# Ending the products ahead of two norms token tile by token tile, in a fused transformer kernel on one core

## The reference

```python
# layer 0, for latent and context tokens (4 token tiles)
h = h + g1 * ((y_conv, y_attention) @ w_out)
h = h + g2 * swiglu(rms_norm(h, norm2_g) * (1 + sc2) + sh2)   # the norm "f"
# layer 1
a = rms_norm(h, norm1_g) * (1 + sc1) + sh1                    # the norm "o"
p = a @ w_in      # cq, dq for 2 token tiles; ck, cv, dk, dv for 4
swiglu(x) = (silu(x @ w1) * (x @ w3)) @ w2                    # hidden width 2816
```

## Time and profile before

| | |
|---|---|
| runs shown | 2064.36 us median of 3 (2060.88 to 2065.09) |
| the profiled execution | 2061.86 us, span 2060.0 us |
| mean granted clock of TensorE | 0.902 |
| busy, share of the span: PE, PEld, DVE, ACT, POOL | 87%, 72%, 60%, 40%, 6% |

### The profile page before, as it was taken

How to read it: one execution, slowest core, us unless ns; L and a number is a source line. 1 busy time by engine, 2 the same in 40 slices (tenths; PEclk the granted TensorE clock), 3 DMA queues, 4 the chain that set the end, 5 groups by cost and what they waited for, 6 DMA issues and landing times. The chain is left out here.

```text
span 2060.0 us, 21353 instructions
## 1 busy us (share of the span) xinstructions
PE 1789.2 (87%) x8622; PEld 1485.9 (72%) x8622; DVE 1246.3 (60%) x1716; ACT 823.7 (40%) x996; POOL 116.7 (6%) x116
## 2 busy tenths in 40 slices
PE   4988999699799995859767999999987899878997
PEld 2766777487678884749646888888867866668986
DVE  5455782377545535554636888888875555555643
ACT  5222231422113224222314777677744433525532
POOL 1310001000100011320010000000000000000000
PEclk8897988799999997975676999999998999998999
DMA  6322331255545432210033888888855521125552
GB/s 277 102 102 93 132 125 39 102 189 184 194 158 204 163 113 73 84 67 13 1 137 109 326 324 332 324 325 324 322 197 179 176 93 40 62 94 194 183 194 102
DMA packets 61146, 332.54 MB, mean 161 GB/s; under 512 B 16804, under 2 KB 17379, under 8 KB 27890
## 3 DMA queue, kind: packets, MB, share of 16 engines
q1 hardware_dynamic: 55792, 321.54, 42.8%
q10 hardware_dynamic: 4354, 6.32, 0.9%
q0 software_dynamic: 896, 3.26, 0.4%
HBM read 329.96 MB, written 1.13 MB: 161 GB/s over the span
## 5 line engine op out<-in xcount | busy, mean ns | idle before, releaser
L1840 DVE TENSOR_TENSOR wlo__69<-raw__68,whi__70 128x2048 fp32r<-128x2048 f32 (+3 forms) x64 | 136.1, 2127 | 93.4 <-ACT whi__70 L1339 93.4
L1840 DVE TENSOR_TENSOR wlo__65<-raw__64,whi__66 128x2048 fp32r<-128x2048 f32 (+4 forms) x55 | 123.4, 2244 | 76.3 <-ACT whi__66 L1339 76.3
L1840 DVE TENSOR_TENSOR wlo__61<-raw__60,whi__62 128x2048 fp32r<-128x2048 f32 (+4 forms) x56 | 108.6, 1939 | 86.2 <-ACT whi__62 L1339 86.2
L1339 ACT ACTIVATE whi__70<-raw__68 128x2048 fp32r<-128x2048 f32 (+3 forms) x64 | 114.1, 1783 | 115.1 <-DMA raw__68<-in_ffn_w 47.9
L1339 ACT ACTIVATE whi__66<-raw__64 128x2048 fp32r<-128x2048 f32 (+4 forms) x55 | 100.0, 1818 | 77.0 <-DMA raw__64<-in_ev_w_in 21.6
L1339 ACT ACTIVATE whi__62<-raw__60 128x2048 fp32r<-128x2048 f32 (+4 forms) x56 | 91.2, 1628 | 72.8 <-DMA raw__60<-in_ev_w_in 20.7
L2757 POOL TENSOR_TENSOR keep__58<-keep__58,keep__59 128x1 f32<-128x1 f32 (+3 forms) x48 | 45.4, 948 | 1199.3 <-DVE keep__58 L1912 1199.3
L1339 ACT ACTIVATE whi__141<-raw__139 128x2048 fp32r<-128x2048 f32 (+2 forms) x16 | 28.1, 1754 | 126.9 <-DMA raw__139<-in_ffn_w 126.9
L860 PE MATMUL ps<-ffn__120,wlo__140 128*128 128x512 f32 x176 | 70.3, 399 | 9.8 <-DVE wlo__140 L1840 7.0
L1840 DVE TENSOR_TENSOR wlo__140<-raw__139,whi__141 128x2048 fp32r<-128x2048 f32 (+2 forms) x16 | 33.5, 2092 | 72.5 <-ACT whi__141 L1339 72.4
L2095 DVE TENSOR_REDUCE keep__58<-ps 128x1 f32<-128x256 f32 (+1 forms) x104 | 56.6, 544 | 28.5 <-PE ps L862 21.7
(11 more groups left out here) (1069 smaller groups left out, 5376.7 us busy)
## 6 DMA issues: line engine op xcount, KB each, us to landing
raw__217<-in_moe_w SPq DMA_DIRECT2D x24, 1024.0 KB, 6.6
raw__221<-in_moe_w SPq DMA_DIRECT2D x24, 1024.0 KB, 6.7
raw__225<-in_moe_w SPq DMA_DIRECT2D x16, 1024.0 KB, 5.7
raw__68<-in_moe_w SPq DMA_DIRECT2D x16, 1024.0 KB, 6.3
raw__64<-in_moe_w SPq DMA_DIRECT2D x16, 1024.0 KB, 6.8
raw__60<-in_ada_w SPq DMA_DIRECT2D x15, 1024.0 KB, 5.8
raw__64<-in_ada_w SPq DMA_DIRECT2D x15, 1024.0 KB, 5.7
raw__68<-in_ffn_w SPq DMA_DIRECT2D x14, 1024.0 KB, 4.9
```

The lines of the kernel that those rows point to most:

```text
L1339: e.activation(t.hi(), t.raw(), ACT.Copy).then_inc(*did("hi", i))
L1840: e.tensor_tensor(t.lo(), t.raw(), t.hi().bitcast(F32), ALU.subtract).then_inc(*did("lo", i))
```

## The change

- The second halves of the output projection and of block 1's ff2 are made by `proj_by_token`: token by token, over all row blocks, with all weight tiles of the half held. The weight tiles become free at the last token.
- The norm's steps follow each token (`norm_by_token` on ACT, likewise in DVE's and POOL's order), with `ahead` at 1 until the first pass is over. Four buffers for scaled tokens instead of two.
- TensorE turns the first two tokens, begins the next stage with them, and turns the other two later: in the FFN the first pair of tiles is made in two halves of 256 tokens (`feat_halves`), in the odd mixer the second turning goes between cq and dq.
- Products wait for the pass by row block (`normed(N, p, k)`).
- The banks come from rings "x" (0 to 3) and "y" (4 to 7) there.
- The 11 small DMAs go to after the FFN's last ff3 product, the tables and the lambda to between the two halves of the last ff2, ACT's Exp in front of the second norm.
- `slot_f` is opened after the first pair of tiles. `in_use` tells the planner the oldest tile still held at an event.

```diff
-        "f": dict(after=("o", 0), free=[("prod", "o", 0, 1, 3), ("res", ("o", 0), 1, 3)],
-                  xs=XSf * 2, tm=TMf, out=AT4f, tiles=4, mod=[
+        "f": dict(after=("o", 0), free=[("prod", "o", 0, 1, 3)], xs_free=[("pv", "a0", 31)], xs=XSf, tm=TMf, out=AT4f, tiles=4, mod=[
...
         busy = max([i for i in range(max(n - 4, 0), n) if not TILES[i].sums], default=0)
+        busy = min([busy] + [in_use[event] for event in events if place[event] == n])
...
-    def normed(N, p):
-        return [(f, N, p, k0) for k0 in range(0, KT, 2) for f in ("nhi", "nlo")]
+    def normed(N, p, k):
+
+        return [(f, N, p, k - k % 2) for f in ("nhi", "nlo")]
...
+        def proj_by_token(key, x, nt, K, src, n, ready, ring):
+
+            kc, tiles = 2048 // n, []
+            for t in range(nt):
+                b = take(ring, *key, t)
+                for k in range(K):
+                    if t == 0 and k % kc == 0:
+                        tiles.append(use(src[k * 128:min(k + kc, K) * 128, :], min(kc, K - k), n))
...
+                    p = mm3(b[:, 0:n], x(k, t), sub((hi, lo), slice(None), k % kc), k == 0, k == K - 1)
+                    if t == nt - 1 and k % kc == kc - 1 and k < K - 1:
+                        p.then_inc(*done("part", *key, k - k % kc))
+                        consumed(tile, "part", *key, k - k % kc)
+                p.then_inc(*done("prod", *key, t))
+            consumed(tiles[-1][0], "prod", *key, nt - 1)
...
+        def feat_halves(parts, x, m, ready, ring, between):
...
+            for half in range(2):
+                o = slice(half * 256, half * 256 + 256)
+                if half:
+                    between()
+                for n, (key, src, f0) in enumerate(parts):
+                    if half == 0:
+                        held.append((*use(src[:, f0 * 128:(f0 + m) * 128], KT, m * 128),
+                                     [take(ring, *key, j) for j in range(m)]))
...
+                    if half:
+                        consumed(tile, "prod", *key, m - 1)
...
+        norm_turn("f", 0, "x")
...
+                feat_halves([(("ff1", 0, 0), W["ffn_w1"][0][:, bs], 0), (("ff3", 0, 0), W["ffn_w3"][0][:, bs], 0)], AT4f, 2,
+                            lambda half, k: normed("f", half, k), "7", lambda: norm_turn("f", 1, "y"))
...
+        norm_turn("o", 0, "x")
         for c0, w_, kind in ODD:
+            if kind == "dq":
+                norm_turn("o", 1, "y")
...
+        def norm_by_token(N, key):
+            at["ahead"] = 1
             for t in range(4):
-                feed(("prod", "o", 0, half, t))
...
+                feed(("prod", *key, 1, t))
+                if t < 3:
+                    norm_square(N, t)
+                if t == 1:
+                    norm_scale(N, 1)
+            norm_turned(N, 0)
+            at["ahead"] = 2
+            norm_square(N, 3)
+            norm_scale(N, 3)
+            norm_turned(N, 1)
...
         for s, n in due(("lam_s",)):
             e.wait_ge(s, n)
         e.activation(LM[:, 2:4], LM[:, 0:2], ACT.Exp).then_inc(*did("lam_e"))
+        norm_by_token("o", ("ff2", 1))
...
             for half in range(2):
+                if blk and half:
+                    for v in range(2):
+                        gain("n1b", sc1b, v, 6, 7)
+                    tables()
+                    at["ahead"] = 1
                 for t in range(4):
                     feed(("prod", "ff2", blk, half, t))
...
+                    if blk and half and t < 3:
+                        norm_scale("o", t)
         norm_turned("o", 0)
+        at["ahead"] = 2
         norm_scale("o", 3)
         norm_turned("o", 1)
```

More of the change, by code:

```diff
@@ L380, in _build @@
     A30 = A3.col
-    XSo, TMo = A3.some(2, 1024), A3.some(3, 512)
+    TMo = A3.some(3, 512)
+    assert A3.col <= slot_f_end
     A3.col = A30
@@ L534, in _build @@
         w["out_free"] = w["tm_free"] = w["free"]
-        w["xs_free"] = lambda t, N=N, w=w: w["free"] + ([("nt", N, 0, 6)] if t > 1 and w["tiles"] == 4 and N != "a" else [])
+        w.setdefault("xs_free", w["free"])
     def xn(N, t):
@@ L801, in done @@
             if book.counting:
-                place[name, *key] = state["tile"]
+                n = place[name, *key] = state["tile"]
+                in_use[name, *key] = next((i for i in range(max(n - 8, 0), n) if TILES[i].done is None), n)
             return did(name, *key)
@@ L896, in feat @@
                 for k in range(KT):
-                    for s, n in state["due"](*ready):
+                    for s, n in state["due"](*ready(k)):
                         e.wait_ge(s, n)
@@ L931, in gates @@
                         for k in range(k0, k0 + 4):
-                            for s, m_ in state["due"](*normed("s", 0)):
+                            for s, m_ in state["due"](*normed("s", 0, k)):
                                 e.wait_ge(s, m_)
@@ L1342, in norm_square @@
             w = NORM[N]
-            for s, n in due(*h_done(w["after"], t), *w["xs_free"](t)):
+            for s, n in due(*h_done(w["after"], t), *w["xs_free"]):
                 e.wait_ge(s, n)
@@ L1530, in scalar_program @@
                          *([("prod", "ff2", 0, 1, 3)] if blk else ()))
-            for half in range(2):
+            for half in range(1 if blk else 2):
                 for t in range(4):
                     feed(("prod", "ff2", blk, half, t))
-        over = [("prod", "ff2", 1, 1, 3)]
-        feed(*over)
-        for s, n in due(*over, ("res", ("ff2", 1), 1, 3), ("fhl", 1, 10)):
+        for s, n in due(("prod", "ff3", 1, 10, 0)):
             e.wait_ge(s, n)
@@ L2237, in vector_program @@
         for half in range(2):
+            if half:
+                for v in range(2):
+                    gain("n2a", sc2, v, 3, 4)
+                at["ahead"] = 1
             for t in range(4):
@@ L2244, in vector_program @@
                 empties(("o", 0, half, t), ("rt", ("o", 0), half, t))
-        for v in range(2):
-            gain("n2a", sc2, v, 3, 4)
-        norm_scale("f", 0)
-        norm_scale("f", 1)
+                if half and t < 3:
+                    norm_scale("f", t)
         norm_turned("f", 0)
-        norm_scale("f", 2)
+        at["ahead"] = 2
         norm_scale("f", 3)
@@ L2796, in gpsimd_program @@
                 residual(("o", 0), half, t, TMPa[(half * 4 + t) % 4])
-        for t in range(4):
-            norm_rsqrt("f", t)
+                if half:
+                    norm_rsqrt("f", t)
         for blk in range(2):
@@ L2804, in gpsimd_program @@
                     residual(("ff2", blk), half, t, TMPf[t])
-        for t in range(4):
-            norm_rsqrt("o", t)
+                    if blk and half:
+                        norm_rsqrt("o", t)
         TS5 = TS.rearrange("p (g i q h f) -> p g i q h f", g=4, i=2, q=2, h=2)
```

131 lines of the change are left out of this document (65 added, 66 removed).

## The result

| | before | changed |
|---|---|---|
| median of the runs on one chip | 2063.7 us (2060.88 to 2065.09, 4 runs) | 2033.5 us (2031.96 to 2038.01, 4 runs) |
| ratio of the times, 95% interval | | 0.986 [0.985, 0.988] |
| the profiled execution | 2061.86 us, span 2060.0 | 2032.86 us, span 2031.0 |
| mean granted clock of TensorE | 0.902 | 0.911 |

The change saves 30 us (29.0 in the spans of the two profiled executions). The predicted time was 2038.4 in a range of 2027 to 2050; it was built on the profiled execution (2061.9 less 23.5), so it compares with the 2032.86 of this table.

The account below looks back on a forecast made before the run. TensorE was taken to be held by chains of dependent steps at two norms, not a full engine. Gains of 13.8 and 15.5 less a 5.8 stall make 23.5 us: 2061.9 to 2038.4, range 2027 to 2050.

Parts of the forecast that it names:

- First head: From the last output product (time E) to the third FFN tile: 52.1 us before, 38.3 forecast, gain 13.8, bounds 10 to 18.
- token 3's square, root and scale come after it, 3.7 us: Ahead of the FFN: after the norm pass on two tokens (E+6.8), token 3 is scaled by E+10.5.
- Second head: From the last ff2 product (E') to dv's first: 60.7 us before, 45.2 forecast, gain 15.5, bounds 11 to 19.5.
- The third held tile: Last ff2 half: its conversion waits for tables and Exp; 3.5 us stall plus 2.3 cold start, cost 5.8, bounds 0 to 9.
- Row blocks "elsewhere 0, at most 1": At the other norms, the first product starts after its weight's low part, so waiting by row block gains 0, at most 1 us.
- The split "is nearly free": First FFN pair in halves: 192 products at 0.114, 21.9 us, against 96 at 0.227, 21.8.
- The sum: Whole kernel: gains 13.8 and 15.5 less cost 5.8 make 23.5 us, from 2061.9 to 2038.4.
- Cold starts: Rival, chance 0.12: three or four short gaps per head; three more cold starts at 2.3, 6.9 us, giving 2045.
- the rule that the prediction weighed: Waits between matmuls put TensorE at its low clock, so one long gap cut into several short ones can cost more.
- No stall at the third held tile: Rival, chance 0.14: if ACT converts that tile first, nothing waits in the last ff2 half; 2032.6.
- Tokens that fall behind on DVE: Rival, chance 0.07: conversions push two tokens past the end of the products, 2 x 4.9 us comes back; 2048.
- The slower case: Rival, chance 0.07: shared in-order DMA queue makes each of 21 later FFN pairs late by 1.5, 31.5 us lost; 2070.

Follow-up runs that it names:

- the run with both turnings together: Changed kernel with the second turning of the odd mixer's norm put back ahead of cq: 2033.3 us, dv 45.1 us after the last ff2 product.
- the two runs that undo it: Changed kernel with ACT's Exp put back behind the second norm: 2029.1 us; then DVE's tables also moved behind the third held tile's low part: 2027.2 us.
- the kernel with the first norm's part alone: Kernel before plus only the first norm's part; ff2, second norm, tables and small DMAs as before: 2039.3 us, ratio 0.989.
- the Exp late: Changed kernel with only ACT's Exp put back behind the second norm: 2029.1 us, ratio 0.984 to the kernel before.

## Why the prediction was right, and where it was off

**First head: 16.2 instead of 13.8.** The order of events was as told: tokens 0 to 2 hidden under the products, pass 1 to E+6.3 (told: 6.8), then token 3, then ff3's conversion, then the second half. The term that was mis-sized is "token 3's square, root and scale come after it, 3.7 us". It is 2.3: ACT is done with its part of the pass at 367.2 and squares token 3 while DVE still makes the last low part, so the scaling ends at E+8.6 instead of E+10.5, and ff3's low part at E+12.7 instead of E+14.7. These 2 us, 0.5 of them from the pass itself, run through to the end of the pair (E+36.1 against E+38.3, E now being 361.65; its first product on 256 columns was at E+3.5, told within 5). Two smaller things beside it: the last terms of the sum (29.1, 3.4 and 5.5) give E+38.0 and not 38.3, and the products of 256 columns come 0.120 us apart here, not 0.114 as in the earlier trace rows. The same in the second head: token 3 at E'+12.5, not 14.1, but there the fourth weight tile ends last and the early token gives nothing.

**Second head: 15.3 instead of 15.5.** First od tile's conversion at E'+0.2 (told 0.2), pass 1 to 10.3 (10.4), fourth tile landed at 20.6 (20.5), pass 2 to 30.1 (30.4), dv at 45.4 (45.2). The statement behind it, that the load of the fourth tile holds the second pass, is shown by the run with both turnings together, where the pass is moved out of its way and dv doesn't come earlier.

**The third held tile: 5.4 (5.9 by the products' starts) instead of 5.8.** The wait is 3.95 with 1.5 of low clock behind it; told were 3.5 and 2.3. So the sum is right because two terms miss in opposite ways. The wait is longer because the tables, told as 3.95 from before, took 5.04 in their new place beside POOL's addition; DVE came to them 0.4 earlier than told. And one thing wasn't in the prediction, though harmless: the tile lands not 4.2 us after its issue, as before, but 8.5, beside the 11 small DMAs. ACT would have been ready at 730.9 and waited for the Exp anyway. In the two runs that undo it this half is 3.4 and 5.9 us shorter.

**Row blocks "elsewhere 0, at most 1": right as far as a trace shows.** In the two heads they are worth 2.7 and 3.0 us, and the forecast had them in its terms for the passes. The median leaves 3.8 us more open, which the profiled execution doesn't have behind its second head.

**The split "is nearly free": nearly right.** Its 192 products, at 0.120 us, are 23.0 us against 21.8 for 96 whole ones, where the prediction had 21.9. It also brings nearly nothing in the first head as the change has it, 0.6 us, and nothing in the second (0.3 the other way). The prediction let a reader think that the half tiles hide the conversion; they do, but the work that is hidden would have fitted behind it.

**The sum: 29.0 instead of 23.5.** 2.4 of the 5.5 are the first head's, mostly token 3's term, 0.2 the two others together, and 2.9 lie where nothing was told: 0.7 before the first head, 0.2 in the FFN and 2.0 behind the second, of which one shorter wait is 1.1. That is within what unchanged code varies by from kernel to kernel, so this part is luck and not a term that the prediction lacked.

**The rivals.** Cold starts: the sum charged three low-clock stretches at 2.3 each, 6.9, and these three cost 5.4 (1.4 in the first head, 1.5 behind the stall, 2.5 at cq). A fourth, 2.3 at dv's first products, was there before too, with 2.5. Together 7.7 us, against 5.7 in the same places before; 1.5 of these 2 us are the stall's, which is a new wait, and only 0.5 come with the gaps cut in pieces. So the rule that the prediction weighed (the Trainium skill, "TensorE: Matmul & The Clock Gate", section "Loop structure matters more than you think") agrees with this trace in part: the low clock follows the waits of 2.42, 3.95 and 5.60 us, and none follows those of 1.62, 0.56 and 1.57 (in the kernel with the first norm's part alone it follows such a pair, 1.57 and 0.56). The 6.9 more of the cold rival are not there. No stall at the third held tile: ruled out by the wait itself, though the rival's time, 2032.6, is what the profiled execution took (2032.9); the time alone would have pointed to it. Tokens that fall behind on DVE: they were 3.8 us behind at token 0 (gate product at 349.16, its last product at 345.3) and had caught up at token 3 (362.05, 0.4 after E). The slower case, weight tiles late through the in-order queue: the FFN took 331.1 against 331.3. (The prediction counts 21 later pairs there; there are 11, of two tiles each, so 31.5 is the price of a delay for each tile.)

## What to carry to other kernels

When a chain of dependent steps stands between two dense stages, end the stage ahead of it piece by piece, and then ask of each engine's queue what stands in front of the step that ends last: here a 0.2 us Exp held a weight tile, a weight tile held token 3's half, and a chain held products that didn't need it. The reordering of the products won 30 us, and moving four such items of the queues won 16 more. An experiment that undoes one part must leave the assignment of buffers as it is; where the planner gave a tile to another slot, that alone cost 7 us. And single gains are best read from the stretch that was edited, as unchanged stretches move by 2 to 4 us between kernels and are counted in each gain.

## What the runs showed of the hardware

Small transfers beside a large one: the 768 KB load of the third ff2 tile took 8.5 us from issue to landing where the same size took 4.2 elsewhere in the same execution. The DMA issues of the changed kernel:

```profile
raw__64<-in_ffn_w SPq DMA_DIRECT2D x1, 768.0 KB, 4.2
raw__60<-in_ffn_w SPq DMA_DIRECT2D x1, 768.0 KB, 8.5
```

11 small DMAs of ACT are issued from 714.8 to 720, the last of them of 256 KB, the load at 720.81. In all eleven other kernels that have them there it took 7.6 to 8.7 us; in the one with the first norm's part alone, where they come after the FFN, 4.1, and before the change 4.2. Which of the 11 slows it, was not tested.

A small product of DVE (128x32) that started 0.08 us after POOL's addition of 128x512 lasted 1.28 us and ended with it, where its 31 neighbours took 0.18 to 0.20. It is so (1.28 to 1.30) in all eight kernels in which the tables stand right behind the last gate product, and in none of the other six (no product above 0.20). Why, was not tested.

The low clock did not come with the first product after every gap. Behind the wait of 3.95 us the products start 0.23 us apart, and only 1.2 us later they fall to 0.43, for eight of them:

```profile
739.33 0.39 PE L867 MATMUL ps<-wlo__61,ffn__129 128*128 128x512 f32 x1
739.56 0.59 PE L868 MATMUL ps<-whi__62,ffn__129 128*128 128x512 f32 x1
739.95 0.63 PE L866 MATMUL ps<-whi__62,ffn__130 128*128 128x512 f32 x1
740.37 0.63 PE L867 MATMUL ps<-wlo__61,ffn__129 128*128 128x512 f32 x1
```

After the 5.60 us ahead of cq the low pitch starts at once, as it did in the earlier trace rows. And behind the 2.23 us that are left of the same stall with the Exp late there is none: but for the first, 0.31, the products there stay 0.22 to 0.24 us apart. Which of these a gap brings was not settled.
